# Layer 0's mixer: gate and value columns first, convolution taps between later steps, weights loaded on SyncE's queue

## What is computed (the reference)

```python
z = h @ w_in                                            # 1024 -> 3080 columns
glu = z[..., :D_A] * jax.nn.sigmoid(z[..., D_A:o1])     # value and gate, 512 each
ca, new_buf_a = _causal_dwconv(glu, buf_a, conv_a_w)    # 31 taps
ya = jax.nn.silu(_layernorm(ca + conv_a_b, ln_a_g, ln_a_b))
qkv, new_buf_qkv = _causal_dwconv(z[..., o1:o2], buf_qkv, conv_qkv_w)   # 4 taps
...                                                     # silu, l2norm of q and k
od, s_new = _gated_delta(q, k, v, g, beta, s0)
od = _rmsnorm(od, gdn_norm_g) * jax.nn.silu(gate.astype(jnp.float32))
mixed = jnp.concatenate([ya, od], axis=-1)
return mixed @ w_out, new_buf_a, new_buf_qkv, s_new
```

## Time and profile before

| | us |
|---|---|
| median of 3 runs | 2352.38 (2351.0 to 2361.53) |
| the profiled execution | 2358.02, span 2356.2 |
| layer 0 mixer's first column | 21.03 |
| the lanes' first "cross" matmul | 108.70 |
| first matmul of the first tail | 324.33 |
| first gather of the first tail | 357.37 |

### The profile page before, as it was taken

How to read it: one execution, slowest core, us unless ns; L and a number is a source line. 1 busy time by engine, 2 the same in 40 slices (tenths; PEclk the granted TensorE clock), 3 DMA queues, 4 the chain that set the end, 5 groups by cost and what they waited for, 6 DMA issues and landing times. The chain is left out here.

```text
span 2356.2 us, 25516 instructions
## 1 busy us (share of the span) xinstructions
PE 1977.2 (84%) x8902; PEld 966.3 (41%) x8902; DVE 1298.6 (55%) x3308; ACT 757.8 (32%) x2225; POOL 653.9 (28%) x650
## 2 busy tenths in 40 slices
PE   7799779887788888866999999989887788888765
PEld 5578645442233332222435654555443233332221
DVE  4485948666667766654100311038666667766754
ACT  3200014343334434433111221124343344434443
POOL 0000004443344354331010000104443444444441
PEclk9897789998999999977999999999999999999977
DMA  9999959999999999997997787828999999999995
GB/s 316 370 333 352 363 194 362 427 426 428 427 427 427 423 405 427 427 427 283 384 392 266 275 308 303 311 112 337 427 427 427 426 427 427 426 427 427 427 427 228
DMA packets 123903, 874.97 MB, mean 371 GB/s; under 512 B 19742, under 2 KB 29726, under 8 KB 38775
## 3 DMA queue, kind: packets, MB, share of 16 engines
q0 software_dynamic: 92160, 662.74, 67.5%
q1 hardware_dynamic: 30751, 198.03, 23.0%
q10 hardware_dynamic: 864, 12.58, 1.4%
HBM read 861.99 MB, written 118.81 MB: 416 GB/s over the span
## 5 line engine op out<-in xcount | busy, mean ns | idle before, releaser
L1570 PE MATMUL tail_acc<-tail_ring,tail_diag 128*128 128x512 f32 x1248 | 617.5, 623 | 131.8 <-ACT tail_diag L1417 130.7
L1717 POOL DMA_INDIRECT tail_ring<-in_peer_uv,tail_idx x348 | 364.9, 1049 | 862.3 <-PE tail_acc L1570 452.6
L1296 DVE CUSTOM_DVE_ANT_0 tail_ring<-tail_ring,all_h 128x1024 f32<-128x1024 f32 x348 | 424.2, 1223 | 261.2 <-DMA tail_ring<-in_peer_uv,tail_idx 259.1
L1570 PE MATMUL tail_acc<-mid_wring,tail_diag 128*128 128x512 f32 x800 | 391.7, 621 | 70.9 <-ACT tail_diag L1417 70.7
L1570 PEld LDWEIGHTS tail_acc<-tail_ring,tail_diag 128*128 128x128 f32 x1248 | 221.4, 193 | 504.0 <-ACT tail_diag L1417 323.2
L1296 DVE CUSTOM_DVE_ANT_0 mid_wring<-mid_wring,all_h 128x1024 f32<-128x1024 f32 x228 | 278.6, 1224 | 172.3 <-DMA mid_wring<-in_peer_uv,tail_idx 172.0
L1409 ACT ACTIVATE tail_gelus<-tail_dots 128x1 f32<-128x1 f32 x576 | 116.4, 202 | 722.5 <-DVE tail_dots L1296 722.1
L1717 POOL DMA_INDIRECT mid_wring<-in_peer_uv,tail_idx x228 | 251.0, 1101 | 319.6 <-PE tail_acc L1570 267.1
L1838 PE MATMUL mix_acc<-mid_wring,all_hT 128*128 128x512 f32 x576 | 273.8, 611 | 1.5 <-PEq L80 1.4
L1570 PEld LDWEIGHTS tail_acc<-mid_wring,tail_diag 128*128 128x128 f32 x800 | 143.8, 194 | 301.8 <-ACT tail_diag L1417 181.5
L1417 ACT ACTIVATE tail_diag<-all_ident,tail_weights 128x128 f32<-128x128 f32 x512 | 205.5, 401 | 24.3 <-PE tail_acc L1570 7.8
(11 more groups left out here) (399 smaller groups left out, 2017.0 us busy)
## 6 DMA issues: line engine op xcount, KB each, us to landing
mid_wring<-in_w_qkv SPq DMA_DIRECT2D x18, 2048.0 KB, 8.9
mix_ring<-in_kT POOLq DMA_DIRECT2D x16, 1024.0 KB, 9.6
mix_ring<-in_v_rows POOLq DMA_DIRECT2D x16, 1024.0 KB, 9.7
out_kv_s<-in_cache_kv_w SPq DMA_DIRECT2D x8, 2016.0 KB, 69.1
mix_ring<-in_kT POOLq DMA_DIRECT2D x16, 768.0 KB, 11.2
mix_ring<-in_v_rows POOLq DMA_DIRECT2D x16, 768.0 KB, 8.6
mid_wring<-in_w_ab ACTq DMA_DIRECT2D x4, 2048.0 KB, 27.2
tail_w_big<-in_w_query SPq DMA_DIRECT2D x8, 1024.0 KB, 11.3
```

Source lines behind the costliest of these rows:

```text
L1296: V.tensor_tensor_reduce(out=u, in0=u, in1=h[:, g, :], scale=1.0, scalar=0.0, op0=ALU.mult, op1=ALU.add, accum_out=dots[:, n:n + 1]).then_ ...
L1570: last = mm(acc[g][:, c * 512:(c + 1) * 512], diag[:, n % DIAGS, :], v[:, c * 512:(c + 1) * 512], start=first, stop=final)
L1717: pool.indirect_dma_start(slot(r), None, table, bass.IndirectOffsetOnAxis(ap=idx[:, j, i:i + 1], axis=0)).then_inc(landed[r], 16)
```

## The change

Four things. The weight columns are laid out anew on the host: gate and value columns alternate at the front, then q, k, v, then the four "out" columns. All columns but the last two go through `column(j)` ahead of the lanes; the last two stand in `branch()` with keys 7.5 and 10.5. DVE's taps are handed out one by one with `tap(n)`, ahead of the lanes and inside `convolve`; the sample half of the taps goes to GpSimd, which multiplies windows and adds them up in a tree. The weight slices 2 to 5 and `w_out` are issued by SP, each when TensorE has finished four more columns, and the cache copies stand between them in small numbers. In the first tail, the loads that SP issued at its start are issued by ScalarE. Some tiles are made narrower, and `intraT` is three tiles now.

```diff
-                roll(4)
-                sp.dma_start(S0[:].rearrange("p b h n -> p (b h n)"), T["state_rows"]).then_inc(state_in, 16)
+                for s in range(2, 6):
+                    sp.wait_ge(col_ready, 4 * (s - 1))
+                    sp.dma_start(wring[:, s % 2], T["w_ab"][:, s]).then_inc(w_in[s % 2], 16)
+                    if s == 2:
+                        sp.dma_start(S0[:].rearrange("p b h n -> p (b h n)"), T["state_rows"]).then_inc(state_in, 16)
+                        roll(2)
+                    else:
+                        roll(3)
                 sp.dma_start(T["out_conv_a_s"][0, :, 0:26, :], T["state_conv_a"][0, :, 4:30, :]).then_inc(stored, 16)
-                roll(16)
+                for half in range(2):
+                    sp.wait_ge(col_ready, 20 + 4 * half)
+                    sp.dma_start(wring[:, half], T["w_out0"][:, half]).then_inc(w_out_in[half], 16)
+                    roll(2)
                 sp.wait_ge(tail_q_out, 3)
...
+                    if j >= 2:
+                        kind, c = JOBS_A[j - 2]
+                        pe.wait_ge({"gate": sig_done, "value": glu_done, "qkv": z_ready, "out": gate_done}[kind], c + 1)
...
+OUT_KEYS = {22: 7.5, 23: 10.5}
...
+                    for j, key in OUT_KEYS.items():
+                        yield key
+                        column(j)
...
+                    pool.wait_ge(glu_done, c + 1)
+                    ch(G.tensor_tensor(windows[:], shifted, taps_of, ALU.mult))
+                    terms = windows[:].rearrange("p b t k -> p (b t) k")
+                    ch(G.tensor_tensor(terms[:, :, 0:15], terms[:, :, 0:15], terms[:, :, 16:31], ALU.add))
+                    for n in (8, 4, 2):
+                        ch(G.tensor_tensor(terms[:, :, 0:n], terms[:, :, 0:n], terms[:, :, n:2 * n], ALU.add))
...
+                def tap(n=1):
+                    for _ in range(n):
+                        if not taps:
+                            return
+                        c, k = taps.pop(0)
...
+                            dve.wait_ge(dve_steps, tapped[c])
+                            ch.step(STT(out=ca[:, c, 0:SEQ], in0=pa[:, c, k:k + SEQ], scalar=wa[:, c, k:k + 1],
+                                        in1=ca[:, c, 0:SEQ], op0=ALU.mult, op1=ALU.add))
...
-                convolve(0)
+                glu(0)
+                tap(6)
                 begin(dve, "gates", "ab dve")
...
+                if not last_layer:
+                    first_loads(act)
                 root("ffn", 0)
```

More of the change, by code:

```diff
@@ L223 @@
 QC = [4, 5, 6, 7, 0, 1, 2, 3, 8, 9, 10, 11]
+AB_COLUMNS = [4, 0, 5, 1, 6, 2, 7, 3] + [8 + n for n in QC] + [20, 21, 22, 23]
 def conv_delta_phase(nc, K, T, wring, w_in, w_out_in, mixT, rolls):
@@ L244, in conv_delta_phase @@
     EXPS, MAIN = at[0, "exps act"], 40
-    job_key = lambda j, half: 5.5 + 1.15 * (2 * j + half)
-    JOBS_A = [(kind, c) for c in range(4) for kind in ("gate", "value")] + [("out", c) for c in range(4)]
-    MEAN_KEY = MAIN + 10.5
+    JOBS_A = [(kind, c) for c in range(4) for kind in ("gate", "value")]
+    JOBS_A += [("qkv", i) for i in range(12)] + [("out", c) for c in range(4)]
+    FIRST_QKV, FIRST_OUT = 8, 20
+    OUT_KEYS = {22: 7.5, 23: 10.5}
+    TAILS_KEY = 13.5
+    MEAN_KEY = 20.5
     class Lanes:
@@ L514, in branch @@
                 def branch():
[L516 to L536, removed]
+                    for j, key in OUT_KEYS.items():
+                        yield key
+                        column(j)
+                    yield TAILS_KEY
                     pe.wait_ge(last_a_ready, 2)
@@ L617, in _ @@
                 q_tails(2)
+                column(21)
                 lanes.run()
@@ L884, in branch @@
-                    c = 0
-                    for i in range(len(taps)):
-                        while c < 4 and tap_key(i) > job_key(2 * c + 1, 1) + 0.2:
-                            yield job_key(2 * c + 1, 1) + 0.2
-                            glu(c)
-                            c += 1
-                        yield tap_key(i)
-                        tap(i)
+                    key = at[0, "cross pe"]
+                    yield key
+                    while taps:
+                        tap(4)
+                        key += 0.5
+                        yield key
@@ L963, in _ @@
                 TT(gt[:], gt[:], ab[:, :, 4:8], ALU.max).then_inc(turn["gates"], 1)
-                convolve(1)
+                tap(13)
+                glu(1)
+                tap(6)
                 begin(dve, "gates", "g dve")
@@ L968, in _ @@
                     op1=ALU.mult).then_inc(turn["gates"], 1)
-                convolve(2)
+                tap(10)
+                glu(2)
+                tap(6)
                 lanes = Lanes([tile(0), tile(1), tile(2), branch(), main()])
                 lanes.run(at[0, "wide pe"])
-                convolve(3)
+                tap(8)
+                glu(3)
                 lanes.run(at[0, "cross pe"])
-                for i in range(4, 11):
+                for i in range(11):
                     convolve(i)
```

235 lines of the change are left out of this document (115 added, 120 removed).

## The result

| | before | after |
|---|---|---|
| median | 2355.85 us (4 runs, 2351.0 to 2361.53) | 2419.84 us (4 runs, 2417.98 to 2421.76) |
| ratio | | 1.0271, 95% interval 1.0242 to 1.03 |
| the profiled execution's span | 2356.2 us | 2420.0 us |
| first matmul of the first tail | 324.33 us | 386.19 us |
| first gather of the first tail | 357.37 us | 420.57 us |

The change costs 64 us, and in the two profiled executions 63 of them are there by the first gather of the first tail. The forecast was 2400, with a range from 2365 to 2420: the direction and the cause were right, the size was too small by 16 to 20 us.

What follows compares the result with a forecast made beforehand. The mixer was taken as bound by arithmetic, with DMA copies done only 19 us sooner. 54 us of dry time put the last copy at 362 and the tail at 373, 49 us later: 2352.4 became about 2400, range 2365 to 2420.

Steps and rivals of the forecast that it cites:

- Full engines, a list of copies as a second clock: Layer 0 mixer: 43 cache copies of about 81 MB fill the DMA engines beside the arithmetic, ending only 19 us sooner.
- Pace of the columns: Ahead of the lanes: a column with its sum every 4.6 us instead of 6.3; column 23 ends at 176.
- The arithmetic ends near 310, 14 us sooner: Mixer stage: fewer columns and tap waits after the last tile's "P" let the arithmetic end 14 us sooner.
- GpSimd's sample taps are hidden: Mixer: the sample half of the taps, 20 us of DVE work, goes to GpSimd, whose additions would be hidden.
- Dry time: SP's queue up to column 23: DMA engines idle 15, 3, 3 and 33 us, 54 in all.
- Rate behind the wait: After column 23: 64.8 MB at 350 GB/s take 185 us, so the last copy lands near 362.
- The stores behind the copies: Mixer's end: delta stores wait behind the copies on SP's in-order queue, need 9 us; tail begins at 373, 49 later.
- The first rival: Mixer's end: stores get past the copies, which run on beneath the tail; +22 us, 2374, chance 0.09.
- The tail's loads on ScalarE's queue: First tail: early loads issued by ScalarE instead of SP; nothing gained or lost, as both queues are empty then.
- Faster copies: Second rival, mixer: copies exceed 350 GB/s, at most 427, so the tail begins at 340.5; +16 us, 2368, chance 0.06.
- The arithmetic's gain arriving: Third rival, mixer and first tail: stores pass the copies and the gathers lose nothing; 14 us faster, 2338, chance 0.07.
- No change: Fourth rival, mixer: column 23 ends by 130, so no dry stretch opens and the time stays; chance 0.04.

Runs made afterwards that it cites:

- e1_fed: Changed kernel with the same cache copies and state load handed out so that SP's queue never runs dry; 2356.9 us, ratio 0.999.
- e2_gap: Changed kernel with eight copies instead of two behind the first half of w_out, filling only the longest dry stretch; 2385.28 us, ratio 1.0118.
- e6_nocopy_after: Changed kernel with the 43 cache copies of this stage left out; 2343.62 us, against 2353.88 for the kernel before without them.
- e10_fed_hold4: e1_fed with its last 4 copies issued behind the eight sample-state stores; 2348.86 us, ratio 0.9949.
- e13_fed_tail3: e1_fed with its last 3 copies held back until the tail's first loads have landed; 2347.73 us, ratio 0.9958.
- e12_wide_sp: Changed kernel, stores still on SP's queue, each sample-state store as 128 rows of 2 KB instead of 512 of 512 bytes; 2420.22 us, ratio 1.0259.
- e3_stores: Changed kernel with the stores of the mixer's last results issued by ScalarE instead of SP; 2420.87 us, ratio 1.0255.
- e14_whole_act: e3_stores with the prompt's state store as 128 rows of 2 KB and all sample states as one store of 128 16 KB rows; 2403.46 us, ratio 1.0177.
- e4_loads_sp: Changed kernel with the first tail's early loads on SP's queue again; 2418.92 us, ratio 1.0253.
- e9_hold11: Changed kernel with the last 11 of its 43 copies issued behind the eight sample-state stores; 2404.56 us, ratio 1.0194.
- e11_wide_act: e3_stores with each sample-state store as 128 rows of 2 KB, the prompt's store left as it was; 2419.54 us, ratio 1.0258.

## Why the prediction was right, and what it sized too small

*Full engines, a list of copies as a second clock.* Right. `e1_fed` and `e2_gap` show that the time follows the dry stretches one to one.

*Pace of the columns.* Right: 4.6 us foretold, and two consecutive sums of squares stand 4.66 us apart (84.72 and 89.38). The lanes began at 145.4 (143), "P" of the last tile came at 172.5 (172), column 23 ended at 179 (176).

*The arithmetic ends near 310, 14 us sooner.* The end was right: 307 for TensorE's last product before the barrier, and 309 to 311 for the tail where nothing else held it (`e6_nocopy_after`, `e10_fed_hold4`, `e13_fed_tail3`). The gain of the stage measured with both kernels freed of copies was 10.6 us; with the scatter named above, 14 can't be excluded.

*GpSimd's sample taps are hidden.* Right as far as the trace shows: 24 us of work between 28 and 145 us, the last of it at 75. After that GpSimd idles 47.88 us until ScalarE brings the input of its copies for the tail rows at 122.79, and no wait of another engine up to 180 us is put down to it. No run takes this part out by itself.

*Dry time.* The first term that was too small. I had 15 + 3 + 3 + 33 = 54 us; the windows show 65. The ends were good (10.9 us up to 44 and 2.6 up to 61 for the 15, 35 from 145 to 180 for the 33). The error lies between: I gave the stretches from 61 to 117 us 6 us and they had 15.3. Two things make it. The columns came later than I had them by 3 to 6 us at each issue (64.07, 84.82, 103.46, 122.10 against 61, 80, 98.5, 116.5), mostly before 85 us. The small products between them took about what I had counted, but TensorE also waited, which I had put at nothing:

```profile
53.27 0.36 PE L456 MATMUL mix_banks<-mix_g,mix_masks 128*128 128x4 f32 x2 [2.42 <-DVE mix_g L975]
...
76.77 8.03 PE L420 MATMUL mix_banks<-all_hT,mid_wring 128*128 128x288 f32 x32 [1.46 <-ACT mix_sample_q L633]
```

And the two columns from 54.59 us took 9.46 us in place of 8.03, at a granted clock of 0.85 from 54.6 to 64. Second, the smaller transfers ran faster than my 350 GB/s (a slice landed in 7.3 us in the median, against 27.2 beside copies), so each small batch was done sooner: 272 GB/s at a share of 0.70 is an estimated 389 while anything moved.

*Rate behind the wait.* The second term, and the one that set the landing. I took 350 GB/s and wrote that little else ran in that stretch; that reading was wrong, for 6.3 of the 53.2 MB from 150 to 302 us were slices of `w_out` and `w_ab` on ScalarE's queue. Copies nearly by themselves made 329 to 335 in the changed kernel and 326 to 335 in `e1_fed`; why they are slower alone isn't shown. I had reached 362 by two sums, and each is put right by itself. From the issue: 178 + 185 was in fact 179.2 + 198.6 = 377.8, so that 1 us comes from column 23 and nearly all the rest from the rate (65.2 MB moved from 180 to 376 us, at 332 GB/s, where I had 64.8 MB at 350). From the dry time: 305.6 + 54 was in fact 305.6 + 65 + 7. The dry time between 61 and 117 us is in the second sum only: with 13 copies handed out ahead of column 23 whatever happens, bytes that move faster there just leave a longer gap. The tail began at 386, not at 373, because 8 us lay between the last landing and it, where I had 11.

*The stores behind the copies.* The outcome was right, and the runs fit a queue of SP that keeps its order: `e12_wide_sp`, whose sample stores have a quarter as many rows, gained nothing. But I took the place on the queue for the whole reason, and that was wrong. On the other queue they were just as late (`e3_stores`). The first rival, "the stores get past them", would have needed few packets as well as another queue; `e14_whole_act` has both, and its tail begins 37 us sooner with copies under way. Even then its time is 2403, not the 2374 that I gave this rival, since the tail's loads are the next to stand beside the copies. I had priced the copies beneath the tail as filled dry time and had not asked what they do to its small loads.

The Trainium skill, "DMA: Bandwidth & Descriptors", section "Queues, rings and completion order", says that each engine goes round the queues that have work, one whole packet at a time. The trace agrees on the turns: 194 packets against 192, 431 against 430. The Trainium skill also gives a packet as some 9 to 17 descriptors. What the profile counts as a packet was one row of 512 bytes in the stores, and may not be the same unit; but with 28 of these against 29 in 4 us on 16 engines, fewer than two from each queue on an engine, turns of nine or more don't fit, and on that point the trace decides. I had read that section for its sentence on completion order alone.

*The tail's loads on ScalarE's queue: nothing.* Right for this kernel (`e4_loads_sp`): its last copy lands at 377.8 and the loads are issued from 386 on. I had bounded the other case by 27.2 us for one load; `e9_hold11` shows 66 us of issues held up for the set.

*Rivals.* Faster copies: refuted by 329 to 335 GB/s. The arithmetic's gain arriving: 10.3 us without copies, and 9 to 10 in the two versions that feed the queue and get stores and loads out of the copies' way. No change: its condition (column 23 before 130) wasn't met, but a near relative is true, the same order with a fed queue, 2356.9.

## What to carry to other kernels

When background transfers fill the engines for a whole stage, count them as a second critical path: before the queue that issues them comes to a wait, it must have put enough bytes in flight to outlast that wait. Put stores and loads that a barrier or the next stage needs where no large transfer is pending, or give them few and long rows; another queue alone didn't help them here. And sum from the last wait on: the time of that issue, the bytes that stand behind it, and the rate that such transfers reach with little beside them (here 332 GB/s and not 350).

## What the hardware showed that I had not expected

With two queues at work the engines moved equal numbers of packets from each: 566 and 592 in 76 us, 194 and 192 in 27 us, 431 and 430 in 61 us. A copy's packets held 64 KB, apart from the small ones, and a store's 512 bytes, so that the prompt's store of 256 KB took about as long beside copies as 25 MB of these (`e11_wide_act`). It fits the 27.2 us of a 2 MB slice with 16 KB rows beside copies, against 7.3 us where the queue was dry.

An issue instruction itself can be held when much is pending: eight stores took 6.43 us to issue with little ahead of them and 87.19 with copies ahead; 28 copies took 46.11. How much may be pending wasn't measured. The last 17 copies that `e1_fed` issues in this stage landed at most 121.8 us after their issue and took 0.6 us each to issue, at most 1.2; the last two of the changed kernel landed 157.6 and 161.0 us after theirs and took 7.5 and 8.8 us. While SP has nothing else to issue, this costs nothing by itself. On ScalarE it delays the activations that stand behind (`e9_hold11`).
